# Forgetting attention of the prompt: spreading the inverse row sums by DRAM and GpSimd in place of TensorE and VectorE

## Chip, core and metric

The kernel runs on one core of one Trainium2 chip. The metric is device time in microseconds (us) of one execution; lower is better. TensorE is called PE, VectorE DVE, ScalarE ACT, GpSimd POOL and the queue that starts most of the transfers SP.

## What is computed

A two-layer decoder step for 2048 prompt tokens and 8 x 4 sample tokens. The change lies in layer 0, in the prompt's forgetting attention, with 8 heads of width 128. For one head and one block of 128 queries:

```python
s = (q_i @ k.T) * scale + (c_i[:, None] - c_keys[None, :])   # c: running sum of log forget gates
s = where(kpos <= qpos, s, -inf)
p = softmax(s, axis=-1)                                      # exp(s - max) / row sum
mix = p @ v
# later, for all heads:  b = concat(mix, memory_attention) * silu(gate);  x = x + rmsnorm(b @ w_out)
```

## The kernel before

The program is a row of stages: the input projection of layer 0 with much else run beside it, a barrier, the function `fox_attention` (lines 518 to 822), a barrier, the output projection, then layer 1. `fox_attention` holds all five engines; each runs its own list of instructions in order and waits on semaphores.

**The loop.** All engines walk the same steps x (`steps`, L562). Step x makes the scores of query block `qs` = x (128 queries; 16 blocks per head, 128 in all), transposes the probabilities of block `qt` = x-2, and multiplies with v for a pair J of query blocks (256 queries), one half of the keys per step: the product of pair J is made in steps 2J+4 and 2J+5. There are 8 pairs per head and 64 in all. A block q of a head sees q+1 blocks of keys, in pieces of 512 keys, so a head's first steps are short and its last are long.

- PE, in each step and piece: three matmuls for the scores (L700, L701, L702: high and low halves of q and k in fp32r), a mask matmul in the last piece (L704), its share of the product with v (L722, full fp32, two passes in the trace for each), then up to four transposes (L737, fp32). The scores go to four PSUM banks in turn.
- DVE: the decay row once in four blocks (L802), one add-and-max per piece out of PSUM (L811), the negated maximum (L816), and at the end of an even step x = 2J+2 the inverse of pair J's row sums (L821: `rr`, one number per query, the queries lying on the partitions, two columns).
- ACT: copies of the transposed probabilities (L762), the exponential with its row sum (L769), and the rounding of the next head's q and k (L750).
- SP: the transfers, in the order of L640 to L651. Stores and the next gate wait for DVE's `mix` (L624, L619), loads of q and k wait for the low halves (L601).
- POOL: the low halves of k (L663) and the work below.

**How the inverse gets to the gates.** The product lies with channels on the partitions and queries along the free axis, so it must be multiplied with 1/row sum along the free axis, the same in every partition. POOL writes a diagonal block from `ident` and `rr` (L670, `dg`), rounds it (L675, `dg_hi`) and takes the rest (L677, `dg_lo`). After the last L722 of a pair, PE multiplies a matrix of ones with both (L727, L728), which leaves the inverses in all 128 partitions of PSUM, in the second half of the bank of the product. At the start of step 2J+6 DVE multiplies the gate with this (L790) and then with the product (L795, `mix`). The buffers of `rr`, `gate`, `mix`, the transposed probabilities and the product are two deep.

```python
for x in range(NS_ + LAG + 2 * QB + 1):        # LAG = 2, QB = 2
    yield (x, qs, qt, product, pair(LAG), pair(LAG + 2 * QB))
```

Of the kernel before, what the change touches and what calls it, by code (L numbers as in the profile page):

```python
# [6 lines left out]
F32 = mybir.dt.float32  # L7
F32R = mybir.dt.float32r
# [506 lines left out]
    return Work(STEPS, plan, dict(sp=sp, pool=pool, pe=pe, act=act, dve=dve))  # L515


def fox_attention(nc, const, banks, zT, cT, bT, v_out):

# [2 lines left out]

    ident, ones_r, ident_b, mask_b = (const[n] for n in ("ident", "ones_r", "ident_b", "mask_b"))
    QB, NB, LAG, CK = 2, 3, 2, 4
    QW, CC = QB * P, 512
    NCH = NQ // QB  # L530
# [1 line left out]
    pieces = [(q + 4) // 4 for q in range(NQ)] * FH  # L532
    first = [sum(pieces[:n]) for n in range(NS_ + 1)]
    S_BANKS, T_BANKS = banks[0:4], banks[4:6]
    OUT = [(banks[6 + n][:, 0:QW], banks[6 + n][:, QW:2 * QW]) for n in range(2)]
    with ExitStack() as s:
        c = Core(nc, s, "fa")
        raws = [c.sb(f"{n}_raw", [P, 2, CC]) for n in "qk"]
# [6 lines left out]
        gate, mix = c.sb("gate", [P, 2, QW]), c.sb("mix", [P, 2, QW])  # L545
        mx, nm = c.sb("mx", [P, NB, 4]), c.sb("nm", [P, NB])
        rs, rr = c.sb("rs", [P, 2, QB]), c.sb("rr", [P, 2, QB])
        dg = c.sb("dg", [P, QB, P])
        dg_hi, dg_lo = (c.sb(n, [P, QB, P], F32R) for n in ("dg_hi", "dg_lo"))
        raw_in = [[c.sem(f"{n}_loaded{u}") for u in range(2)] for n in "qk"]  # L550
        v_in = [[c.sem(f"v{u}_loaded{ch}") for ch in range(CK)] for u in range(2)]
        hi_d, lo_d = [c.sem(f"{n}_hi_done") for n in "qk"], [c.sem(f"{n}_lo_done") for n in "qk"]
        c_in, dec_d = c.sem("c_loaded"), c.sem("decay_ready")
        g_in, mix_out = ([c.sem(f"{n}{u}") for u in range(2)] for n in ("gate_loaded", "mix_stored"))
        s_done, s_used, nm_d, p_done = (c.sem(n) for n in ("scores_done", "scores_used", "maxima_ready", "exp_done"))
        t_done, tc_d, rr_d = (c.sem(n) for n in ("p_transposed", "pT_copied", "row_inverse_ready"))
        dg_d, dgl_d, r_done, o_done = (c.sem(n) for n in ("diagonals_made", "diagonals_split", "inverse_spread", "pv_done"))
        gr_d, mix_d = c.sem("gate_scaled"), c.sem("mix_ready")
        block = s.enter_context(nc.Block())
        his, los = (q_hi, k_hi), (q_lo, k_lo)  # L560
# [1 line left out]
        def steps():  # L562

            for x in range(NS_ + LAG + 2 * QB + 1):
                pair = lambda lag: (x - lag) // QB if x >= lag and (x - lag) % QB == 0 and (x - lag) // QB < NJ else None
                yield (x, x if x < NS_ else None, x - LAG if LAG <= x < NS_ + LAG else None,
                       divmod(x - LAG - QB, QB) if LAG + QB <= x < NS_ + LAG + QB else None,  # L570
                       pair(LAG), pair(LAG + 2 * QB))

        def splits(x):

# [20 lines left out]
        def _(sp):  # L595
# [19 lines left out]
            def gates(J):  # L615
# [2 lines left out]
                    sp.wait_ge(mix_d, J - 1)  # L618
                sp.dma_start(gate[:, J % 2, :], zT[3 * D + XW + h * P:3 * D + XW + (h + 1) * P, QW * j:QW * (j + 1)]).then_inc(g_in[J % 2], 16)  # L619

            def store(J):
                h, j = divmod(J, NCH)
                sp.wait_ge(mix_d, J + 1)
                sp.dma_start(bT[h * P:(h + 1) * P, QW * j:QW * (j + 1)], mix[:, J % 2, :]).then_inc(mix_out[J % 2], 16)  # L624
# [12 lines left out]
                load_v(1, ch)  # L637
            for J in range(2):
                gates(J)
            for x, qs, qt, product, jr, jm in steps():  # L640
                for n, h, ch in splits(x - 1) if x else []:
                    i = CK * h + ch + 2
                    if i < CK * FH:
                        load(n, i // CK, i % CK)
                if qs is not None and qs % NQ == NQ - 2 and qs // NQ + 1 < FH:
                    decays(qs // NQ + 1)
                h, ch = divmod(x - LAG - 2 * QB - 1, NQ)
                if 1 <= h < FH - 1 and ch % 2 == 0 and ch // 2 < CK:
                    load_v(h + 1, ch // 2)
                if jm is not None:  # L650
                    store(jm)  # L651
                    if jm + 2 < NJ:
                        gates(jm + 2)
# [3 lines left out]
        @block.gpsimd  # L657
        def _(pool):
            def split(n, h, ch):
                i = CK * h + ch  # L660
                at = part(n, h, ch)
                pool.wait_ge(hi_d[n], i + 1)
                nc.gpsimd.tensor_tensor(los[n][at], raws[n][:, i % 2, :], his[n][at].bitcast(F32), ALU.subtract).then_inc(lo_d[n], 1)  # L663
            for n, h, ch in splits(-1):
                if n:
                    split(n, h, ch)
            for x, qs, qt, _, J, jm in steps():
                if J is not None:
                    pool.wait_ge(rr_d, J + 1)
                    nc.gpsimd.tensor_tensor(dg[:, :, :], ident[:, :].unsqueeze(1).broadcast_to([P, QB, P]),  # L670
                                            rr[:, J % 2, :].unsqueeze(2).broadcast_to([P, QB, P]), ALU.mult).then_inc(dg_d, 1)
                    pool.wait_ge(dg_d, 2 * J + 1)
                    if J:
                        pool.wait_ge(r_done, J)
                    nc.gpsimd.tensor_copy(dg_hi[:, :, :], dg[:, :, :]).then_inc(dg_d, 1)  # L675
                    pool.wait_ge(dg_d, 2 * J + 2)
                    nc.gpsimd.tensor_tensor(dg_lo[:, :, :], dg[:, :, :], dg_hi[:, :, :].bitcast(F32), ALU.subtract).then_inc(dgl_d, 1)  # L677
                    pool.wait_ge(dgl_d, J + 1)
                for n, h, ch in splits(x):
                    if n:  # L680
                        split(n, h, ch)

        @block.tensor
        def _(pe):
            for x, qs, qt, product, _, _ in steps():
                n_parts = max(1, parts(qs, qt))
                for p in range(n_parts):
                    if qs is not None and p < pieces[qs]:
# [17 lines left out]
                    if product is not None:  # L706
                        J, half = product
                        h, j = divmod(J, NCH)
                        n_keys = QB * (j + 1) // 2

                        late = 1 if half == 0 and n_parts > 1 else 0
                        at, of = max(0, p - late), n_parts - late
                        shared = range(n_keys * at // of, n_keys * (at + 1) // of) if p >= late else ()
                        for n in (n_keys * half + y for y in shared):
                            if n == 0:
                                if J >= 2:
                                    pe.wait_ge(mix_d, J - 1)
                                pe.wait_ge(tc_d, first[QB * (J + 1)])
                            if n % 4 == 0:
                                pe.wait_ge(v_in[h % 2][n // 4], 16 * (h // 2 + 1))  # L720
                            c0 = max(0, n - QB * j) * P
                            last = nc.tensor.matmul(OUT[J % 2][0][:, c0:QW], v[:, h % 2, n * P:(n + 1) * P], pT[:, J % 2, n, c0:QW],  # L722
                                                    start=(n == 0), stop=(n == QB * (j + 1) - 1))
                            if n == QB * (j + 1) - 1:
                                last.then_inc(o_done, 1)
                                pe.wait_ge(dgl_d, J + 1)
                                nc.tensor.matmul(OUT[J % 2][1], ones_r[:, :], dg_hi[:, :, :].rearrange("p a n -> p (a n)"), start=True, stop=False)  # L727
                                nc.tensor.matmul(OUT[J % 2][1], ones_r[:, :], dg_lo[:, :, :].rearrange("p a n -> p (a n)"),  # L728
                                                 start=False, stop=True).then_inc(r_done, 1)
                    if qt is not None and p < pieces[qt]:  # L730
                        g, q = first[qt] + p, qt % NQ
                        if p == 0:
# [9 lines left out]
        def _(act):  # L742
# [7 lines left out]
                nc.scalar.activation(his[n][part(n, h, ch)], raws[n][:, i % 2, :], ACT.Copy, scale=SCALE if n == 0 else 1.0).then_inc(hi_d[n], 1)  # L750
            for n, h, ch in splits(-1):
                split(n, h, ch)
            for x, qs, qt, _, _, _ in steps():
                if qt is not None:
                    q, J = qt % NQ, qt // QB
                    for p in range(pieces[qt]):
# [18 lines left out]
        def _(dve):  # L775
# [7 lines left out]
                if n == 0:  # L783
                    split(n, h, ch)
            n_dec = 0
            for x, qs, qt, _, jr, jm in steps():
                if jm is not None:
                    dve.wait_ge(r_done, jm + 1)
                    dve.wait_ge(g_in[jm % 2], 16 * (jm // 2 + 1))
                    nc.vector.tensor_tensor(gate[:, jm % 2, :], gate[:, jm % 2, :], OUT[jm % 2][1], ALU.mult).then_inc(gr_d, 1)  # L790
                    dve.wait_ge(gr_d, jm + 1)
                    dve.wait_ge(o_done, jm + 1)
                    if jm >= 2:
                        dve.wait_ge(mix_out[jm % 2], 16 * (jm // 2))
                    nc.vector.tensor_tensor(mix[:, jm % 2, :], gate[:, jm % 2, :], OUT[jm % 2][0], ALU.mult).then_inc(mix_d, 1)  # L795
                if qs is not None and qs % 4 == 0:
                    h, q = divmod(qs, NQ)
                    w = P * (q + 4)
# [18 lines left out]
                if jr is not None:  # L817
                    dve.wait_ge(p_done, QB * (jr + 1))
                    if jr >= 2:
                        dve.wait_ge(dg_d, 2 * (jr - 1))  # L820
                    nc.vector.reciprocal(rr[:, jr % 2, :], rs[:, jr % 2, :]).then_inc(rr_d, 1)  # L821
                for n, h, ch in splits(x):
                    if n == 0:
# [1472 lines left out]
def decoder_step(nc, ins, outs):  # L2296
# [14 lines left out]
    x1p, x1s = scratch("x1p", (SEQ, D)), scratch("x1s", (NS, D))  # L2311
    cT, sufT = scratch("cT", (FH, SEQ)), scratch("sufT", (DB * FH * TN, PAGES * P))
    cnew = scratch("cnew", (FH, NS))

    with ExitStack() as s:
        banks = [s.enter_context(nc.psum_tensor(f"bank{i}", [P, 512], F32)) for i in range(8)]
# [76 lines left out]
                project_pass(nc, "p0", const, banks, fox_w_in, halves, tiles, z0, bufs, rows,  # L2393
                             [making, norm, kv, sample, gates, fox, prompt, late], (page_table, cache_logf, past, ptab))
        nc.all_engine_barrier()
        fox_attention(nc, const, banks, z0, cT, bT, fox_v_p)
        output_projection(nc, "o0", banks, bT, w_out[0], norm_post[0], xp, xs, x1p, x1s)


# [45 lines left out]
```

## Time and profile before

| | |
|---|---|
| median of 3 runs | 3416.53 us (3413.59 to 3417.41) |
| the profiled execution: its own time | 3418.22 us |
| its span in the profile | 3416.6 us |
| stretch of `fox_attention`'s steps, from its first score to its last `mix` | 1464 to 2064 us |
| PE's busy time over the span | 3257.0 us |

Times in the rows are microseconds from the start of the span unless marked ns. "PEld" is PE's weight loads, which overlap the matmuls. A row "A <- B: t, n, m" of the waits says that A stood idle for t us in n times until B had finished, m at most. The ends of matmuls are modelled, so the distance from one start to the next is the better measure of what a matmul costs.

### The profile page before, as it was taken

The page shows a single profiled execution, that of the slowest core. Times are in us where ns is not written, and L with a number is a line of the kernel's source. Part 1 is how long each engine was busy: PE and PEld are TensorE (multiplying, and loading weights), DVE is VectorE, ACT ScalarE, POOL GpSimd, SP SyncE. Part 2 cuts the span into 40 slices and gives each one's busy share as a digit, 9 for nine tenths or more (in the row PEclk, how much of TensorE's full clock was granted, in tenths as well). Part 3 has the DMA queues.
Part 4 walks back from the last instruction along what each step waited for, and adds up shares of the span by engine and source line. Part 5 has one row for each costly group of instructions (what it writes and reads, how often), then busy time and mean ns, then how long its engine had stood idle before and what let it go on. Part 6 is the DMA issues. An engine that isn't in the chain of part 4 may idle for free. (4 is left out here: it accounts for less than half of the span.)

```text
span 3416.6 us, 51365 instructions
## 1 busy us (share of the span) xinstructions
PE 3257.0 (95%) x19697; PEld 2788.2 (82%) x19697; DVE 1302.6 (38%) x2583; ACT 1098.5 (32%) x2154; POOL 439.8 (13%) x643
## 2 busy tenths in 40 slices
PE   7999999899999999979999998997999999996999
PEld 7999999677777777768888886886999888775887
DVE  4331223232232215445555554223322246655332
ACT  3112232122222225355555553112223244112221
POOL 3310000101111112122222220000000012211000
PEclk9999999999999999989999999998999999998999
DMA  5444533579889964342232206332333444756431
GB/s 159 135 125 135 163 113 112 159 226 305 282 286 314 299 201 142 110 133 84 82 92 87 93 29 193 120 93 89 108 113 105 158 143 142 230 159 198 145 108 55
DMA packets 409059, 514.70 MB, mean 151 GB/s; under 512 B 50760, under 2 KB 298057, under 8 KB 407264
## 3 DMA queue, kind: packets, MB, share of 16 engines
q1 hardware_dynamic: 385975, 443.69, 41.7%
q0 software_dynamic: 22848, 67.78, 6.2%
q8 instruction: 158, 2.59, 0.3%
q14 instruction: 78, 0.63, 0.1%
HBM read 387.52 MB, written 124.22 MB: 150 GB/s over the span
## 5 line engine op out<-in xcount | busy, mean ns | idle before, releaser
L389 ACT ACTIVATE z_st_p<-bank 128x352 f32<-128x352 f32 (+3 forms) x325 | 168.5, 519 | 657.3 <-PE bank L364 657.0
L1522 PE MATMUL bank<-w_hi_o,b_hi_o 128*128 128x512 f32 x816 | 319.7, 392 | 26.9 <-DVE w_lo_o L1581 26.9
L364 PE MATMUL bank<-h00hi,w_hi_p 128*128 128x352 f32 x984 | 325.0, 330 | 4.8 <-DVE h00lo L1042 3.3
L1523 PE MATMUL bank<-w_hi_o,b_lo_o 128*128 128x512 f32 x816 | 318.9, 391 | 0.0
L1524 PE MATMUL bank<-w_lo_o,b_hi_o 128*128 128x512 f32 x816 | 318.9, 391 | 0.0
L364 PE MATMUL bank<-h00hi,w_lo_p 128*128 128x352 f32 x984 | 317.0, 322 | 0.0
L364 PE MATMUL bank<-h00lo,w_hi_p 128*128 128x352 f32 x984 | 316.7, 322 | 0.0
L722 PE MATMUL bank<-pT_fa,v_fa 128*128 128x256 f32 (+1 forms) x1152 | 291.4, 373 | 1.7 <-DVE mix_fa L795 0.7
L364 PE MATMUL bank<-h01hi,w_hi_p 128*128 128x512 f32 x656 | 274.2, 418 | 0.0
L364 PE MATMUL bank<-h01hi,w_lo_p 128*128 128x512 f32 x656 | 258.3, 394 | 0.0
L364 PE MATMUL bank<-h01lo,w_hi_p 128*128 128x512 f32 x656 | 257.2, 392 | 0.0
L321 DVE CAST w_hi_p<-w_raw_p 128x1024 fp32r<-128x1024 f32 (+1 forms) x130 | 89.3, 687 | 413.5 <-PE bank L364 413.4
L811 DVE CUSTOM_DVE_ANT_0 sc_fa<-bank,decay_fa 128x512 f32<-128x512 f32 (+2 forms) x320 | 189.1, 609 | 142.8 <-PE bank L704 82.6
L722 PEld LDWEIGHTS bank<-pT_fa,v_fa 128*128 128x128 f32 x1152 | 206.5, 191 | 28.9 <-DVE mix_fa L795 2.6
L762 ACT COPY pT_fa<-bank 128x512 f32<-128x512 f32 (+2 forms) x320 | 164.2, 518 | 203.5 <-PE bank L737 203.5
L1980 DVE COPY kT_sf<-bank 128x512 f32<-128x512 f32 x128 | 88.6, 692 | 354.2 <-PE bank L1908 354.1
L1522 PEld LDWEIGHTS bank<-w_hi_o,b_hi_o 128*128 128x128 f32 x816 | 154.1, 189 | 61.0 <-DVE w_lo_o L1581 27.8
L364 PEld LDWEIGHTS bank<-h00hi,w_hi_p 128*128 128x128 f32 x984 | 185.6, 189 | 10.4 <-issue 4.9
L364 PE MATMUL bank<-h10hi,w_hi_p 128*128 128x352 f32 x576 | 188.1, 327 | 3.1 <-DVE h10lo L1042 3.1
L364 PEld LDWEIGHTS bank<-h00lo,w_hi_p 128*128 128x128 f32 x984 | 186.0, 189 | 0.6
L364 PE MATMUL bank<-h10lo,w_hi_p 128*128 128x352 f32 x576 | 185.7, 322 | 0.0
L364 PE MATMUL bank<-h10hi,w_lo_p 128*128 128x352 f32 x576 | 185.7, 322 | 0.0
(290 smaller groups left out, 6588.3 us busy)
## 6 DMA issues: line engine op xcount, KB each, us to landing
k_raw_sf<-in_cache_fox_k SPq DMA_DIRECT2D x128, 512.0 KB, 5.4
v_raw_sf<-in_cache_fox_v POOLq DMA_DIRECT2D x128, 512.0 KB, 5.8
z<-z_st_p SPq DMA_DIRECT2D x112, 512.0 KB, 2.8
w_raw_p<-in_fox_w_in SPq DMA_DIRECT2D x80, 512.0 KB, 5.2
b_raw_o<-bT SPq DMA_DIRECT2D x32, 768.0 KB, 6.5
w_raw_p<-in_pool_w_in SPq DMA_DIRECT2D x48, 512.0 KB, 5.0
out<-tok_p SPq DMA_DIRECT2D x64, 256.0 KB, 4.3
w_raw_o<-in_w_out SPq DMA_DIRECT2D x24, 512.0 KB, 4.5
```

The lines of the kernel that those rows point to most:

```text
L321: nc.vector.tensor_copy(w_hi[:, u, :, 0:width], w_raw[:, u, :, 0:width]).then_inc(whi_d, 1)
L364: last = nc.tensor.matmul(bank[:, 0:width], wt[:, u, k, :], h[:, k, at0:at0 + width], start=(m == 0), stop=(m == MM - 1))
L389: nc.scalar.activation(z_st[0:rows_t, t % 2, at0:at0 + width], bank[0:rows_t, 0:width], tiles[t][2]).then_inc(z_read, 1)
L722: last = nc.tensor.matmul(OUT[J % 2][0][:, c0:QW], v[:, h % 2, n * P:(n + 1) * P], pT[:, J % 2, n, c0:QW], start=(n == 0), stop=(n == QB * ...
L762: nc.scalar.copy(pT[:, J % 2, 4 * p:4 * p + nk, a * P:(a + 1) * P], T_BANKS[g % 2][:, 0:nk * P].rearrange("p (n q) -> p n q", q=P)).then_i ...
L811: nc.vector.tensor_tensor_reduce(out=sc[:, b, k0:k0 + w], in0=S_BANKS[g % 4][:, 0:w], in1=decay[:, k0:k0 + w], scale=1.0, scalar=LOWEST, o ...
L1522: nc.tensor.matmul(bank(t, half)[:, :], bh, w_hi[:, k, cols], start=(k == 0), stop=False)
L1523: nc.tensor.matmul(bank(t, half)[:, :], bl, w_hi[:, k, cols], start=False, stop=False)
L1524: last = nc.tensor.matmul(bank(t, half)[:, :], bh, w_lo[:, k, cols], start=False, stop=(k == NK - 1))
L1980: nc.vector.tensor_copy(kT[:, s // 2 % 2, 4:8, s % 2 * P:(s % 2 + 1) * P], T_BANKS[1][:, :].rearrange("p (h n) -> p h n", h=4)).then_inc(k ...
```

## The change

`rr` is stored to a new DRAM scratch `inverses` (8 x 2048) in 256 runs of 4 bytes (step 2J+3, SP), read back as a row of 1 KB into each of the 128 partitions (step 2J+4, SP, behind a wait for the store's landing), and POOL multiplies the gate with it in SBUF (step 2J+5). DVE keeps L795 alone. The three diagonal instructions, the two matmuls with ones and DVE's gate multiply go.

```diff
-    OUT = [(banks[6 + n][:, 0:QW], banks[6 + n][:, QW:2 * QW]) for n in range(2)]
+    OUT = [banks[6 + n][:, 0:QW] for n in range(2)]
...
+        r_bc = c.sb("r_bc", [P, 2, QW])
...
-                       pair(LAG), pair(LAG + 2 * QB))
+                       pair(LAG), pair(LAG + 2 * QB), pair(LAG + 1), pair(LAG + 2), pair(LAG + 3))
...
+            def store_inverse(J):
+                h, j = divmod(J, NCH)
+                sp.wait_ge(rr_d, J + 1)
+                sp.dma_start(inverses[h, QW * j:QW * (j + 1)].rearrange("(a p) -> p a", p=P), rr[:, J % 2, :],
+                             allow_slow_non_contiguous=True).then_inc(r_out[J % 2], 16)
+
+            def spread_inverse(J):
+                h, j = divmod(J, NCH)
+                sp.wait_ge(r_out[J % 2], 16 * (J // 2 + 1))
+                if J >= 2:
+                    sp.wait_ge(gr_d, J - 1)
+                sp.dma_start(r_bc[:, J % 2, :], inverses[h, QW * j:QW * (j + 1)].partition_broadcast(P)).then_inc(r_in[J % 2], 16)
...
-            for x, qs, qt, product, jr, jm in steps():
+            for x, qs, qt, product, jr, jm, ji, jb, _ in steps():
+                if ji is not None:
+                    store_inverse(ji)
+                if jb is not None:
+                    spread_inverse(jb)
...
-                    pool.wait_ge(rr_d, J + 1)
-                    nc.gpsimd.tensor_tensor(dg[:, :, :], ident..., rr..., ALU.mult).then_inc(dg_d, 1)
-                    pool.wait_ge(dg_d, 2 * J + 1)
-                    if J:
-                        pool.wait_ge(r_done, J)
-                    nc.gpsimd.tensor_copy(dg_hi[:, :, :], dg[:, :, :]).then_inc(dg_d, 1)
-                    pool.wait_ge(dg_d, 2 * J + 2)
-                    nc.gpsimd.tensor_tensor(dg_lo[:, :, :], dg[:, :, :], dg_hi..., ALU.subtract).then_inc(dgl_d, 1)
-                    pool.wait_ge(dgl_d, J + 1)
+                    pool.wait_ge(g_in[J % 2], 16 * (J // 2 + 1))
+                    pool.wait_ge(r_in[J % 2], 16 * (J // 2 + 1))
+                    nc.gpsimd.tensor_tensor(gate[:, J % 2, :], gate[:, J % 2, :], r_bc[:, J % 2, :], ALU.mult).then_inc(gr_d, 1)
...
                                 last.then_inc(o_done, 1)
-                                pe.wait_ge(dgl_d, J + 1)
-                                nc.tensor.matmul(OUT[J % 2][1], ones_r[:, :], dg_hi..., start=True, stop=False)
-                                nc.tensor.matmul(OUT[J % 2][1], ones_r[:, :], dg_lo..., start=False, stop=True).then_inc(r_done, 1)
...
-                    dve.wait_ge(r_done, jm + 1)
-                    dve.wait_ge(g_in[jm % 2], 16 * (jm // 2 + 1))
-                    nc.vector.tensor_tensor(gate[:, jm % 2, :], gate[:, jm % 2, :], OUT[jm % 2][1], ALU.mult).then_inc(gr_d, 1)
                     dve.wait_ge(gr_d, jm + 1)
                     dve.wait_ge(o_done, jm + 1)
...
-                        dve.wait_ge(dg_d, 2 * (jr - 1))
+                        dve.wait_ge(r_out[jr % 2], 16 * (jr // 2))
                     nc.vector.reciprocal(rr[:, jr % 2, :], rs[:, jr % 2, :]).then_inc(rr_d, 1)
```

## Rows read from the trace of the kernel before

**Rows 1.** The page: busy time of each engine over the span.
```profile
PE 3257.0 (95%) x19697; PEld 2788.2 (82%) x19697; DVE 1302.6 (38%) x2583; ACT 1098.5 (32%) x2154; POOL 439.8 (13%) x643
```

**Rows 2.** Busy time by stretch; last columns: granted PE clock, DMA share, GB/s.
```profile
1464.00:1500.00 36.00, 27.89 (x158) 23.22 (x159) 21.10 (x72) 21.46 (x45) 13.59 (x18) 0.81 0.57 176
1600.00:1700.00 100.00, 99.22 (x590) 84.60 (x589) 50.33 (x162) 55.30 (x106) 25.20 (x37) 1.00 0.27 79
```

**Rows 3.** Waits from 1464 to 2065 us.
```profile
DVE gate_fa L790 <- PE bank L728: 50.3, 24, 7.5
...
PE bank L737 <- ACT pT_fa L762: 3.2, 6, 0.5
```

**Rows 4.** Groups of instructions by line and shape, 1464 to 2065 us.
```profile
L677 POOL TENSOR_TENSOR dg_lo_fa<-dg_fa,dg_hi_fa 128x256 fp32r<-128x256 f32 x64 | 49.1, 767 | 5.1
...
L728 PE MATMUL bank<-dg_lo_fa,ones_r_const 128*128 128x256 f32 x64 | 18.1, 283 | 0.0
```

**Rows 5.** Timeline, PE: a pair's end before transposes, and a stretch without it.
```profile
2043.61 0.87 PE L722 MATMUL bank<-pT_fa,v_fa 128*128 128x256 f32 x4
...
2044.24 0.36 PE L727 MATMUL bank<-dg_hi_fa,ones_r_const 128*128 128x256 f32 x1
...
2044.56 0.82 PE L737 MATMUL bank<-ident_const,sc_fa 128*128 128x128 f32 x6
...
2052.17 1.03 PE L722 MATMUL bank<-pT_fa,v_fa 128*128 128x256 f32 x4
...
2053.04 0.60 PE L737 MATMUL bank<-ident_const,sc_fa 128*128 128x128 f32 x4
```

**Rows 6.** Timeline, PE: product before scores, without the two matmuls and with them.
```profile
1551.45 0.65 PE L722 MATMUL bank<-pT_fa,v_fa 128*128 128x256 f32 x2
...
1552.17 0.40 PE L701 MATMUL bank<-k_hi_fa,q_lo_fa 128*128 128x512 f32 x1
...
1553.51 0.44 PE L722 MATMUL bank<-pT_fa,v_fa 128*128 128x128 f32 x2
...
1554.26 0.40 PE L701 MATMUL bank<-k_hi_fa,q_lo_fa 128*128 128x512 f32 x1
```

**Rows 7.** Timeline, second head: inverses and mixes of pairs 9 and 10, POOL's k split.
```profile
1552.97 0.17 DVE L821 RECIPROCAL rr_fa<-rs_fa 128x2 f32<-128x2 f32 x1
...
1558.14 1.28 POOL L663 TENSOR_TENSOR k_lo_fa<-k_raw_fa,k_hi_fa 128x512 fp32r<-128x512 f32 x1 [2.27 <-ACT k_hi_fa L750]
...
1558.42 0.17 DVE L821 RECIPROCAL rr_fa<-rs_fa 128x2 f32<-128x2 f32 x1
...
1561.32 0.42 DVE L795 TENSOR_TENSOR mix_fa<-gate_fa,bank 128x256 f32<-128x256 f32 x1
...
1569.21 0.42 DVE L795 TENSOR_TENSOR mix_fa<-gate_fa,bank 128x256 f32<-128x256 f32 x1
```

**Rows 8.** DMA issues of the whole run: count, KB each, median us to landing.
```profile
c_bc_fa<-cT SPq DMA_DIRECT2D x8, 1024.0 KB, 5.4
...
gate_fa<-z SPq DMA_DIRECT2D x64, 128.0 KB, 2.2
bT<-mix_fa SPq DMA_DIRECT2D x64, 128.0 KB, 2.8
...
sc_col_pm<-in_pool_scale SPq DMA_DIRECT2D x1, 4.0 KB, 7.9
```

**Rows 9.** Timeline: the end of the stage.
```profile
2062.39 0.36 PE L727 MATMUL bank<-dg_hi_fa,ones_r_const 128*128 128x256 f32 x1
...
2062.91 0.42 DVE L790 TENSOR_TENSOR gate_fa<-gate_fa,bank 128x256 f32<-128x256 f32 x1 [7.46 <-PE bank L728]
2063.36 0.42 DVE L795 TENSOR_TENSOR mix_fa<-gate_fa,bank 128x256 f32<-128x256 f32 x1
```

**Rows 10.** Timeline, start of the stage: inverse and mix of pair 0, DVE.
```profile
1475.34 0.17 DVE L821 RECIPROCAL rr_fa<-rs_fa 128x2 f32<-128x2 f32 x1
...
1483.20 0.42 DVE L795 TENSOR_TENSOR mix_fa<-gate_fa,bank 128x256 f32<-128x256 f32 x1
```

More of the change, by code:

```diff
@@ L515, in prompt_gates, with fox_attention @@
     return Work(STEPS, plan, dict(sp=sp, pool=pool, pe=pe, act=act, dve=dve))
-def fox_attention(nc, const, banks, zT, cT, bT, v_out):
-    ident, ones_r, ident_b, mask_b = (const[n] for n in ("ident", "ones_r", "ident_b", "mask_b"))
+def fox_attention(nc, const, banks, zT, cT, bT, inverses, v_out):
+    ident, ident_b, mask_b = (const[n] for n in ("ident", "ident_b", "mask_b"))
     QB, NB, LAG, CK = 2, 3, 2, 4
@@ L547, in fox_attention @@
         rs, rr = c.sb("rs", [P, 2, QB]), c.sb("rr", [P, 2, QB])
-        dg = c.sb("dg", [P, QB, P])
-        dg_hi, dg_lo = (c.sb(n, [P, QB, P], F32R) for n in ("dg_hi", "dg_lo"))
+        r_bc = c.sb("r_bc", [P, 2, QW])
         raw_in = [[c.sem(f"{n}_loaded{u}") for u in range(2)] for n in "qk"]
@@ L555, in fox_attention @@
         s_done, s_used, nm_d, p_done = (c.sem(n) for n in ("scores_done", "scores_used", "maxima_ready", "exp_done"))
-        t_done, tc_d, rr_d = (c.sem(n) for n in ("p_transposed", "pT_copied", "row_inverse_ready"))
-        dg_d, dgl_d, r_done, o_done = (c.sem(n) for n in ("diagonals_made", "diagonals_split", "inverse_spread", "pv_done"))
+        t_done, tc_d, rr_d, o_done = (c.sem(n) for n in ("p_transposed", "pT_copied", "row_inverse_ready", "pv_done"))
+        r_out, r_in = ([c.sem(f"{n}{u}") for u in range(2)] for n in ("inverse_stored", "inverse_spread"))
         gr_d, mix_d = c.sem("gate_scaled"), c.sem("mix_ready")
@@ L666, in _ @@
                     split(n, h, ch)
-            for x, qs, qt, _, J, jm in steps():
+            for x, qs, qt, _, _, _, _, _, J in steps():
                 if J is not None:
-                    pool.wait_ge(rr_d, J + 1)
-                    nc.gpsimd.tensor_tensor(dg[:, :, :], ident[:, :].unsqueeze(1).broadcast_to([P, QB, P]),
-                                            rr[:, J % 2, :].unsqueeze(2).broadcast_to([P, QB, P]), ALU.mult).then_inc(dg_d, 1)
-                    pool.wait_ge(dg_d, 2 * J + 1)
-                    if J:
-                        pool.wait_ge(r_done, J)
-                    nc.gpsimd.tensor_copy(dg_hi[:, :, :], dg[:, :, :]).then_inc(dg_d, 1)
-                    pool.wait_ge(dg_d, 2 * J + 2)
-                    nc.gpsimd.tensor_tensor(dg_lo[:, :, :], dg[:, :, :], dg_hi[:, :, :].bitcast(F32), ALU.subtract).then_inc(dgl_d, 1)
-                    pool.wait_ge(dgl_d, J + 1)
+                    pool.wait_ge(g_in[J % 2], 16 * (J // 2 + 1))
+                    pool.wait_ge(r_in[J % 2], 16 * (J // 2 + 1))
+                    nc.gpsimd.tensor_tensor(gate[:, J % 2, :], gate[:, J % 2, :], r_bc[:, J % 2, :], ALU.mult).then_inc(gr_d, 1)
                 for n, h, ch in splits(x):
@@ L684, in _ @@
         def _(pe):
-            for x, qs, qt, product, _, _ in steps():
+            for x, qs, qt, product, *_ in steps():
                 n_parts = max(1, parts(qs, qt))
@@ L721, in _ @@
                             c0 = max(0, n - QB * j) * P
-                            last = nc.tensor.matmul(OUT[J % 2][0][:, c0:QW], v[:, h % 2, n * P:(n + 1) * P], pT[:, J % 2, n, c0:QW],
+                            last = nc.tensor.matmul(OUT[J % 2][:, c0:QW], v[:, h % 2, n * P:(n + 1) * P], pT[:, J % 2, n, c0:QW],
                                                     start=(n == 0), stop=(n == QB * (j + 1) - 1))
@@ L725, in _ @@
                                 last.then_inc(o_done, 1)
-                                pe.wait_ge(dgl_d, J + 1)
-                                nc.tensor.matmul(OUT[J % 2][1], ones_r[:, :], dg_hi[:, :, :].rearrange("p a n -> p (a n)"), start=True, stop=False)
-                                nc.tensor.matmul(OUT[J % 2][1], ones_r[:, :], dg_lo[:, :, :].rearrange("p a n -> p (a n)"),
-                                                 start=False, stop=True).then_inc(r_done, 1)
                     if qt is not None and p < pieces[qt]:
@@ L752, in _ @@
                 split(n, h, ch)
-            for x, qs, qt, _, _, _ in steps():
+            for x, qs, qt, *_ in steps():
                 if qt is not None:
@@ L785, in _ @@
             n_dec = 0
-            for x, qs, qt, _, jr, jm in steps():
+            for x, qs, qt, _, jr, jm, *_ in steps():
                 if jm is not None:
-                    dve.wait_ge(r_done, jm + 1)
-                    dve.wait_ge(g_in[jm % 2], 16 * (jm // 2 + 1))
-                    nc.vector.tensor_tensor(gate[:, jm % 2, :], gate[:, jm % 2, :], OUT[jm % 2][1], ALU.mult).then_inc(gr_d, 1)
                     dve.wait_ge(gr_d, jm + 1)
@@ L794, in _ @@
                         dve.wait_ge(mix_out[jm % 2], 16 * (jm // 2))
-                    nc.vector.tensor_tensor(mix[:, jm % 2, :], gate[:, jm % 2, :], OUT[jm % 2][0], ALU.mult).then_inc(mix_d, 1)
+                    nc.vector.tensor_tensor(mix[:, jm % 2, :], gate[:, jm % 2, :], OUT[jm % 2], ALU.mult).then_inc(mix_d, 1)
                 if qs is not None and qs % 4 == 0:
@@ L2313, in decoder_step @@
     cnew = scratch("cnew", (FH, NS))
+    inverses = scratch("inverses", (FH, SEQ))
     with ExitStack() as s:
@@ L2395, in decoder_step @@
         nc.all_engine_barrier()
-        fox_attention(nc, const, banks, z0, cT, bT, fox_v_p)
+        fox_attention(nc, const, banks, z0, cT, bT, inverses, fox_v_p)
         output_projection(nc, "o0", banks, bT, w_out[0], norm_post[0], xp, xs, x1p, x1s)
```

## The prediction, made before the changed kernel ran

> **What bounds the kernel now.** I read the page first: PE is busy 95% of the span, no other engine over 38% [rows 1]. Then the table by stretch, since a share of the whole says nothing of one stage. In the attention steps PE is busy 99.2 of 100 us at the full clock, DVE 50, ACT 55, POOL 25, and the DMA share is 0.27 [rows 2]; four further stretches of 100 us look the same. Only the first 36 us are looser (27.9 busy, clock 0.81) [rows 2]. Third, the waits of this stage: the longest waits of DVE for what the change touches, 50.3 us [rows 3], are waits of an idle engine for PE. PE itself waits 3.2 us in six times for ACT's copies, all in short steps [rows 3], and about 8 us once, at the start. So the stage is one long stream of matmuls. What leaves that stream is gained; what leaves DVE and POOL is not, except at the end, where nothing runs beside them.
>
> **What goes from PE.** 64 times L727 and 64 times L728, 283 ns each of the latter [rows 4]. Busy times overlap their neighbours', so I take distances between starts. What follows the two differs.
>
> *Transposes follow (5 of 8 pairs of a head, 40 in all).* From the last run of L722 (two passes of 256 columns and two of 128) to the transposes: 2044.56 - 2043.61 = 0.95 us; L727 begins at 0.63 of it [rows 5]. Without the two, four passes of 256 columns need 2053.04 - 2052.17 = 0.87 us [rows 5], 0.217 each, so the run with half-width passes would need 3 x 0.217 = 0.65. The two matmuls cost 0.95 - 0.65 = 0.30 us.
>
> *Scores follow (3 of 8, 24 in all).* From a half-width L722 over both matmuls and L700 to L701: 1554.26 - 1553.51 = 0.75 us. The nearest case without them has a full-width L722: 1552.17 - 1551.45 = 0.72 us [rows 6]; the half width takes 0.217 off, 0.50. So 0.25 us. It is less than 0.30 because fp32r matmuls start late behind fp32 ones: now L727 pays that, afterwards L700 does.
>
> Sum: the 64th pair is the end of the stage, counted below; 39 x 0.30 + 24 x 0.25 = 11.7 + 6.0 = 17.7 us. As bounds: 0.20 for each (a spacing that the remaining stream gives back in part) makes 12.6, 0.32 for each (start of L727 to start of L737 [rows 5]) 20.2.
>
> **What goes from DVE.** L790, 64 times 0.42 us [rows 9]. It is hidden behind PE and I cost it at nothing; the step's first add-and-max starts some 0.75 us sooner against PE, which can only shrink the 3.2 us of [rows 3].
>
> **The end of the stage.** Nothing covers it. Now: L727 at 2062.39, L790 at 2062.91, L795 at 2063.36 [rows 9]. Afterwards L795 can start when the last L722 is drained, which ends by its neighbours some 0.25 us after 2062.39. So 2063.36 - 2062.64 = 0.7 us. The inverse of that pair is made over 15 us before and will be long there.
>
> **What is added, and whether it stays hidden.** Per pair: a store of 1 KB in 256 runs of 4 bytes, a spread of 128 KB, and one POOL multiply.
> - The multiply: nearest row L677, same size, two inputs in SBUF, 767 ns [rows 4]. POOL loses three instructions for it.
> - The spread: the same bytes and row length as `gate`, 2.2 us; bound above by `c_bc`, eight times larger, 5.4 us [rows 8].
> - The store: bounds are 2.2 us (below, the gate's row) and 7.9 us, the only row with 4-byte runs, `sc_col`, four times as many and issued behind 1.5 MB of loads [rows 8]. I take 2.8, the store of `mix` [rows 8]: that one moves 128 times the bytes, and 16 short runs per engine are few.
> - Issue on SP: about 0.4 us for each of the two.
>
> The Trainium skill speaks against the store: "DMA: Bandwidth & Descriptors", section Specifications, wants at least 512 B per transfer for line rate and says that below it the engines read, modify and write. By that rule this store is of the worst kind. It gives no time, and in this trace I see none for a store of 4-byte runs.
>
> The chain from inverse to gate is then 0.1 + 0.4 + 2.8 + 0.4 + 2.2 + 0.8 = 6.7 us. The room is the time from the end of L821 to L795 of the same pair. It is smallest for the second pair of a head: 1561.32 - 1553.14 = 8.2 us [rows 7]; I walked all 64 pairs: the third of a head has 1569.21 - 1558.59 = 10.6 us [rows 7], the others more; the last head's second has somewhat less room, but no k split before it. POOL does its k split, 1558.14 to 1559.42 [rows 7], ahead of that multiply, so the gate is ready at about 1560.2, just in time. If it comes late, DVE waits at the head of the step with its add-and-max queued behind it; PE goes on through four score banks, and its transposes use blocks two steps old. I put that slack at about 4 us (two short steps of some 2.2 us).
>
> SP's queue: `store_inverse` of J waits for an inverse that DVE makes at the end of the step whose `mix` SP has just stored, so nothing useful is held. `spread_inverse` holds SP for the store's 2.8 us; behind it stand loads of q and k (needed some 7 steps later), the store of the last `mix` (its buffer is needed four steps later) and the next gate (needed three steps later). For pair 10 I get the gate ready at about 1566.8 against 1568.6. No stall.
>
> **The start** is the place where it fails to fit. SP still issues loads of v and gates until 1479, under a DMA share of 0.57 [rows 2]. The first inverse is ready at 1475.5, its `mix` runs at 1483.20 [rows 10]. With the store issued at 1479.0, landing at 1481.7, the spread landing near 1484.6 and the multiply, the gate is there at 1485.4, 2.2 us late. PE's slack covers most of it: I charge 0.5 us, with 0 to 3 as bounds.
>
> **Sum.** 17.7 + 0.7 - 0.5 = 17.9 us; I round it down by half a us for the short steps, where PE waits for ACT anyway, to 17.4. The profiled execution's 3418.22 becomes 3400.8. Its time lies 1.7 us above the median of the runs, 3416.53, so the median becomes 3399.1. About 0.2% (6.8 us) is what a measurement of this kernel can tell from no change; this is 0.51%.
>
> **Rivals.**
> 1. *The short steps are paced by ACT and DVE, not by PE.* Speaks for it: PE's waits for L762 lie there. Against: they sum to 3.2 us in the whole stage, and the chain through DVE gets shorter by more than PE's. Three of eight pairs end in short steps; if theirs is given back, 24 x 0.27 = 6.5 us is lost: 3405.6. Chance 0.12.
> 2. *A slower chain with part of the gain.* Store 5 us, spread 3: 9.7 us against 8.2, DVE late by 1.5 us or more at the second and third pair of each head, and the slack is less than I put it: PE loses about 1 us per head and 2 more at the start, 3399.1 + 10 = 3409. Chance 0.08.
> 3. *Slower: the round trip through DRAM paces the head's first steps.* One mechanism: 4-byte stores land like `sc_col` and the spread like `c_bc`. Chain 0.1 + 0.4 + 7.9 + 0.4 + 5.4 + 1.3 + 0.8 = 16.3 us against 8.2, late by 8.1, of which 4 are slack: 4 us in the second pair; SP is held for 8 us per pair and the third pair, with 10.6 us of room, is late too, some 2 us beyond slack. 6 x 8 = 48 us lost against 17.9 gained: 3447. It decides the sign once the chain is longer than 8.2 + 4 + 17.9/8 = 14.4 us. The trace speaks against it: the DMA share is low and `gate` lands in 2.2 us. This is also how the page's rule would make itself felt; since so few runs are stored, I give it 0.04.
> 4. *The matmuls' places are not gained at all* (the stream is held by weight loads or by the sequencer, so that two fewer change nothing): 3416. PEld is busy 84.6 of 100 us [rows 2], so it isn't the limit. Chance 0.04.
>
> The forecast has the rest, 0.72.
>
> **Range.** Its own spread is 3396.5 (0.32 us for each) to 3404 (0.20). Down to 3395.5 for a gain on PE's waits for ACT, up to 3407 for rival 1 and the start of rival 2: left out are rivals 3, 4 and most of 2. Faster by over 0.2%: forecast, rival 1 and most of 2, 0.90; within 0.2%: rival 4 and the rest of 2, 0.06; slower 0.04.
>
> **What would show it.** L795 of the last pair about 17 us earlier against the stage's first score; PE busy 99% in the same stretches; the period of a head down by 2.2 us; the store landing in 2 to 3.5 us; the second pair's `mix` waiting less than 1 us for POOL. I am wrong if PE shows new idle time at the blocks 6 to 10 of each head, released by ACT or DVE (rivals 2, 3), or if the head's period shrinks by under 1.5 us with PE at 99% (rival 4 or a wrong price for the two matmuls).

## The result, and the profile after

| | before | changed |
|---|---|---|
| median | 3416.95 us | 3617.12 us (3611.33 to 3625.12, 4 runs) |
| profiled execution, span | 3416.6 us | 3617.6 us |

The ratio is 1.0595, 95% interval [1.0582, 1.0608]: 200 us slower, where 17 us faster was forecast.

The page first. The columns are busy time, share of the span and instructions.

```profile
PE 3308.1 (91%) x19569; PEld 2812.3 (78%) x19569; DVE 1263.3 (35%) x2519; ACT 1097.3 (30%) x2154; POOL 371.0 (10%) x515
PEclk9999999999999999788889898899899999997999
```

The 128 matmuls, 64 DVE and 128 POOL instructions are gone, as against [rows 1], but PE's share fell and the granted clock has dips in the attention's slices. The table by stretch of the changed kernel (PE, PEld, DVE, ACT, POOL, clock, DMA share, GB/s) says where:

```profile
1600.00:1700.00 100.00, 79.39 (x413) 65.12 (x414) 34.94 (x120) 42.95 (x80) 10.32 (x12) 0.88 0.55 68
```

In the same stretch PE did 590 matmuls before at clock 1.00 [rows 2], now 413. No engine took its place: all are idle more. The DMA share doubled to 0.55 while the GB/s fell from 79 to 68. So engines wait, and transfers occupy the DMA engines without moving much. The waits of this stage (A <- B: us in total, times, longest), then those of SP's queue:

```profile
POOL gate_fa L687 <- DMA r_bc_fa<-inverses: 698.9, 63, 17.0
DVE mix_fa L797 <- POOL gate_fa L687: 385.7, 62, 10.4
ACT sc_fa L774 <- DVE nm_fa L818: 291.3, 76, 11.5
...
PE bank L709 <- DVE mx_fa L813: 136.8, 38, 9.2
```

```profile
SPq L631 <- DMA inverses<-rr_fa: 588.2, 63, 12.2
SPq L600 <- DVE q_lo_fa L785: 5.0, 2, 4.5
SPq L600 <- POOL k_lo_fa L679: 3.5, 3, 1.7
```

Read from the bottom: SP stood 588 us waiting for stores of the inverses to land (L631 starts the spread); POOL waited for the spread, DVE for POOL, ACT and PE for DVE. SP's waits for the low halves, 8.5 us here, were these in the kernel before:

```profile
SPq L601 <- DVE q_lo_fa L780: 136.8, 28, 7.0
SPq L601 <- POOL k_lo_fa L663: 134.0, 29, 6.6
```

SP is no longer early for anything. PE pays twice. It stands idle, and after an idle time it runs at a lower granted clock: 0.53 from 1806.5 to 1809.4 us, close to the lower of its two levels (1.2 of 2.4 GHz), after 4.4 us without work. The same matmul (L710, 512 columns) at that clock and 4 us later:

```profile
1807.00 0.63 PE L710 MATMUL bank<-k_hi_fa,q_lo_fa 128*128 128x512 f32 x1
...
1810.74 0.39 PE L710 MATMUL bank<-k_hi_fa,q_lo_fa 128*128 128x512 f32 x1
```

The issues of transfers in the stage (count, KB each, median us to landing):

```profile
gate_fa<-z SPq DMA_DIRECT2D x64, 128.0 KB, 8.7
r_bc_fa<-inverses SPq DMA_DIRECT2D x63, 128.0 KB, 5.0
bT<-mix_fa SPq DMA_DIRECT2D x62, 128.0 KB, 8.9
...
inverses<-rr_fa SPq DMA_DIRECT2D x64, 1.0 KB, 10.6
```

One KB needs 10.6 us, and the transfers around it are slow too: `gate` needs 8.7 us, 2.2 before [rows 8]. SP's timeline shows the turn of its list:

```profile
1797.62 0.32 SPq L631 DMA_DIRECT2D r_bc_fa<-inverses  x1
...
1802.37 0.49 SPq L623 DMA_DIRECT2D inverses<-rr_fa  x1
1802.91 0.47 SPq L607 DMA_DIRECT2D v_fa<-out  x1
1811.08 0.33 SPq L631 DMA_DIRECT2D r_bc_fa<-inverses  x1
1811.46 0.43 SPq L636 DMA_DIRECT2D bT<-mix_fa  x1
1811.93 0.43 SPq L618 DMA_DIRECT2D gate_fa<-z  x1
1812.40 0.45 SPq L623 DMA_DIRECT2D inverses<-rr_fa  x1
```

From 1803.4 to 1811.1 SP does nothing. The moment the store has landed it starts the spread, the last product's store, the next gate and at once the next store, whose inverse is long there. The gate is started half a us ahead of the store (1811.93 and 1812.40) and not behind it; it is so with 30 of the 32 gates whose landing the trace tells, and none of the 32 was started while a store was under way. The store holds up what was started just before it as well.

The first `mix` of the stage is at 1491.87, the last at 2268.14: 776.3 us for 63 intervals, 12.3 us per pair, in short steps nearly as in long ones (means of 11.4 to 14.0 us by the pair's place in its head). Before, the pairs took 4.2 to 13.6 us by the length of their steps, 9.2 on average.

### The profile page after: what moved, and what is told of

Read it like the earlier page. It is cut to its first block and busy times, and to the rows that moved or that the text cites. A ratio compares the mean times of both kernels' runs of the same rounds, so it can differ in the third digit from the quotient of the medians.

```text
span 3617.6 us, 50980 instructions
## 1 busy us (share of the span) xinstructions
PE 3308.1 (91%) x19569; PEld 2812.3 (78%) x19569; DVE 1263.3 (35%) x2519; ACT 1097.3 (30%) x2154; POOL 371.0 (10%) x515
## 5 line engine op out<-in xcount | busy, mean ns | idle before, releaser
L731 PE MATMUL bank<-pT_fa,v_fa 128*128 128x256 f32 (+1 forms) x1152 | 307.9, 389 | 1.7 <-issue 0.7
L709 PE MATMUL bank<-k_hi_fa,q_hi_fa 128*128 128x512 f32 (+2 forms) x320 | 159.2, 497 | 150.6 <-DVE mx_fa L813 136.8
L731 PEld LDWEIGHTS bank<-pT_fa,v_fa 128*128 128x128 f32 x1152 | 217.7, 201 | 32.2 <-issue 2.6
L774 ACT ACTIVATE sc_fa<-sc_fa,nm_fa 128x128 f32<-128x128 f32 (+15 forms) x128 | 154.2, 1205 | 291.5 <-DVE nm_fa L818 291.3
L742 PE MATMUL bank<-ident_const,sc_fa 128*128 128x128 f32 x1088 | 187.4, 291 | 18.3 <-ACT sc_fa L774 9.4
L709 PEld LDWEIGHTS bank<-k_hi_fa,q_hi_fa 128*128 128x128 f32 x320 | 68.7, 215 | 164.6 <-DVE mx_fa L813 115.6
```

What stands on the lines that cost most here:

```text
L709: nc.tensor.matmul(out, qh, k_hi[:, h % 2, k0:k0 + w], start=True, stop=False)
L731: last = nc.tensor.matmul(OUT[J % 2][:, c0:QW], v[:, h % 2, n * P:(n + 1) * P], pT[:, J % 2, n, c0:QW], start=(n == 0), stop=(n == QB * (j ...
L742: last = nc.tensor.transpose(T_BANKS[g % 2][:, n * P:(n + 1) * P], sc[:, qt % NB, (4 * p + n) * P:(4 * p + n + 1) * P], ident[:, :])
L774: nc.scalar.activation(sc[:, qs % NB, 0:w], sc[:, qs % NB, 0:w], ACT.Exp, bias=nm[:, qs % NB:qs % NB + 1], accum_out=rs[:, J % 2, qs % QB: ...
```

## Experiments

Two questions. **Why does the store need 10.6 us**: the number of runs, their place in DRAM, or a wait behind other transfers? **Through whom does it cost**: SP's held queue (theory H), the longer chain from inverse to gate (rival R), or the load on the DMA engines (rival C)? Each ratio below is against the kernel before on the same chip.

### Without the store

```diff
-                sp.wait_ge(r_out[J % 2], 16 * (J // 2 + 1))
+                sp.wait_ge(rr_d, J + 1)
...
-                sp.dma_start(r_bc[:, J % 2, :], inverses[h, ...].partition_broadcast(P))...
+                sp.dma_start(r_bc[:, J % 2, :], cT[h, ...].partition_broadcast(P))...
```

> Leaves out the store of the inverses: the spread reads rows of cT instead, so the gates are scaled with wrong numbers; the spread, POOL's multiply and the rest stay. Theory S (the landing of the store, 10.6 us in the trace, for which SP waits with its queue behind it, makes the loss): the time falls to what was predicted, 3399 us, within 4; spreads land in 2.2 us. Rival Q (the spread, POOL's multiply or SP's longer list cost the time whatever the store does): over 3416.

3396.23 us, ratio 0.9944 [0.9928, 0.9961]. All else of the change stays and is worth about what was forecast: 18.6 us against the kernel before on the same chip, 17.4 forecast. The spread landed in 3.9 us, not 2.2, and DVE waited only 0.6 us in all for the scaled gates. The loss comes with the store and the wait for it.

### Runs of 8 bytes

```diff
-inverses[h, ...].rearrange("(a p) -> p a", p=P)
+inverses[h, ...].rearrange("(p a) -> p a", p=P)
```

> The same 1 KB stored as 128 runs of 8 bytes (both queries of a partition side by side in DRAM); POOL reads the spread row in steps of two. Theory S by number of runs: the landing halves to about 5.5 us and the time to 3440 or less. Theory L (what costs is that many engines write into the same 1 KB of DRAM, run by run): the same, 5.5 us. Rival F (the landing is a wait behind other transfers of the queue): unchanged, 10 us and 3617.

3408.26 us, ratio 0.998 [0.997, 0.999]; the store lands in 4.9 us, `gate` in 4.6. The expectation had 3440 or less. Half the runs, less than half the landing; rival F falls. SP still waits 202 us for the store. Number and place are not yet told apart.

### The same runs, apart

```diff
-inverses[h, ...].rearrange("(a p) -> p a", p=P), rr[:, J % 2, :],
+inverses[h, ...].rearrange("(a p s) -> p a s", p=P, s=P)[:, :, 0:1], rr[:, J % 2, :].unsqueeze(2),
```

> Still 256 runs of 4 bytes, but each into a block of 512 bytes of its own in a scratch 128 times as large; the spread waits for it as before but reads a row of cT, so the gates are scaled with wrong numbers. Theory S by number of runs: as the changed kernel, 10 us and 3617. Theory L (writes into the same 1 KB stand in line): the landing falls to about 3 us and the time to about 3402.

3397.82 us, ratio 0.9955 [0.994, 0.9971]. Two closer spacings, s=16 and s=8:

> As the run with the 4-byte runs 512 bytes apart, but 64 bytes apart (a pair's inverses in 16 KB of DRAM); the spread reads rows of cT again, so the gates are scaled with wrong numbers. If the runs stand in line only where they fall into the same 64 bytes: landing near 3 us, time near 3398. If into the same 512 bytes or the same few KB: landing 5 to 10 us, time 3410 to 3617.

> As the run with the 4-byte runs 64 bytes apart, now 32 bytes apart, two in each 64 bytes; the spread reads rows of cT, so the gates are scaled with wrong numbers. If the runs stand in line where they fall into the same 64 bytes, and two per line are few: landing 2.8 to 3.5 us, 3397 to 3402. If a wider block counts: landing over 4 us.

One execution each: 3399.31 us and 3400.53 us. The row of the store was the same in the three kernels; the one with the closest spacing, 32 bytes, beside its `gate`:

```profile
gate_fa<-z SPq DMA_DIRECT2D x64, 128.0 KB, 2.3
...
inverses<-rr_fa SPq DMA_DIRECT2D x64, 1.0 KB, 2.8
```

256 runs of 4 bytes land in 2.8 us, exactly the price taken in the prediction, if each has 32 bytes to itself; eight runs to 32 bytes take 10.6 us, four of 8 bytes 4.9 us. So neither the size nor the number of the runs is slow, but their lying side by side. Theory L holds, in a narrower block than I had expected: 32 bytes apart is enough, and spacings between 8 and 32 bytes were not run, so the width of the block stays open. These three kernels don't read the stored words back; the run with the transpose, below, does.

The trace's records of single DMA packets say where the time is. The 4-byte packets take 9 ns each, crowded or 512 bytes apart (median, and no more in nine of ten). The packets of other transfers are stretched: those of 1 KB (gates, `mix`, spreads) take 139 ns on average in the stage of the changed kernel and 53 with the words 512 bytes apart, those of 512 bytes 78 and 29.

The Trainium skill's rule ("DMA: Bandwidth & Descriptors", Specifications: under 512 B the engines read, modify and write) agrees with the crowded store and would also have condemned the one with 32 bytes between the runs, which lands like a store of 128 KB. That crowded writes wait for one another's read and write back would fit both, but no run shows the mechanism itself.

### The target in SBUF

```diff
-sp.dma_start(inverses[h, ...].rearrange("(a p) -> p a", p=P), rr[:, J % 2, :], ...)
+for a in range(QB):
+    sp.dma_start(row[0:1, J % 2, P * a:P * (a + 1)], rr[:, J % 2, a:a + 1], ...)
```

> The whole computation. The same 256 runs of 4 bytes, in two transfers, go to a row of one partition in SBUF and the spread reads that row; no DRAM. If it is DRAM that makes small writes stand in line: landing 2 to 3 us; the spread reads 128 KB out of one partition and may take 3 to 6 us; time 3397 to 3410. Rival N (the count of runs costs, whatever the target): landing 8 us or more, 3550 or more.

3426.35 us, ratio 1.0038 [1.0024, 1.0051]; the 4-byte writes land in 3.5 us though they are crowded, the spread out of one partition in 6.7 us and `gate` in 6.3. Rival N falls: side by side in SBUF the words are not slow, so the 10.6 us need the target in DRAM. (Two things changed, the target and one transfer made into two; no run has the two transfers to DRAM.) The loss against the other kernels without a slow store is another one, by its rows the spread of 128 KB out of a single partition: it needs more than the 3 to 6 us expected, and DVE waited 83.5 us for POOL's multiply. That it is the spread which slows `gate` here was not run by itself.

### An unused store in the kernel before

```diff
+                if x % QB == 1 and 0 <= (x - LAG - 1) // QB < NJ:
+                    store_inverse((x - LAG - 1) // QB)     # rr four deep, nobody waits but its fourth successor
```

> The kernel before, with the store of 256 runs of 4 bytes added at the same place of SP's list and nobody waiting for its landing (the inverses have four buffers). Theory W (the wait on SP is what costs): 3417 to 3420. Rival C (the slow store holds up the other transfers too, as gate's landing of 8.7 us in the changed kernel suggests): gate lands in 6 us or more, and the time rises to 3425 or more.

3415.23 us, ratio 1.0007 [0.9997, 1.0017]. Here is what it does to the others, in this kernel:

```profile
gate_fa<-z SPq DMA_DIRECT2D x64, 128.0 KB, 8.9
bT<-mix_fa SPq DMA_DIRECT2D x63, 128.0 KB, 8.6
...
inverses<-rr_fa SPq DMA_DIRECT2D x64, 1.0 KB, 9.4
```

Half of each theory: the other transfers are held up as much as in the changed kernel (C's mechanism), yet the time doesn't move (W's time). The transfers start early enough here, because SP doesn't wait: in the whole stage DVE waits 8.2 us for gates.

### The wait moved to POOL

```diff
-                if jb is not None:
-                    spread_inverse(jb)
...
+                    pool.wait_ge(r_out[J % 2], 16 * (J // 2 + 1))
+                    pool.dma_start(r_bc[:, J % 2, :], inverses[h, ...].partition_broadcast(P))...
```

> The changed kernel with one thing moved: the wait for the store's landing and the start of the spread go from SP to POOL, ahead of its multiply; the store stays as it is (256 runs of 4 bytes in 1 KB) and SP waits for no landing. Theory H (SP, held for some 10 us per pair with stores, gates and the next inverse behind it, turns at 12 us per pair whatever the length of the steps): most of the loss goes, 3400 to 3440, and what is left lies at the first pairs of a head, which have 8 to 14 us of room. Rival R (the chain from the inverse to the gate, 10.6 + 5 + 0.8 us, is too long wherever it runs): 3550 or more.

3509.2 us, ratio 1.0281 [1.0257, 1.0305]: between the two expectations, so it decided nothing. Its waits from 1464 to 2065 us, the last one SP's, show why:

```profile
POOL gate_fa L683 <- DMA r_bc_fa<-inverses: 289.6, 54, 9.4
DVE mix_fa L793 <- POOL gate_fa L683: 193.2, 38, 11.4
POOL r_bc_fa L680 <- DMA inverses<-rr_fa: 190.8, 27, 13.9
...
SPq L600 <- POOL k_lo_fa L670: 228.5, 29, 12.6
```

POOL now waits for the landing of the store and then for that of the spread before it multiplies, and DVE waits for POOL: that is rival R's chain. POOL's splits of k come late as well, so that SP waits 228.5 us for them before it reloads the buffer, 134.0 in the kernel before: that may hold SP's queue again. The run has both and doesn't tell them apart.

### DVE without the inverse, and the wait two pairs later

DVE multiplies product and gate when the product is there; POOL multiplies the result with the inverse in step 2J+9, and SP stores it in step 2J+10. The buffers of `rr`, `mix` and the spread row are four deep. The second kernel differs from the first in one number, the step in which SP waits for the store and starts the spread.

```diff
-pair(LAG + 1), pair(LAG + 2), pair(LAG + 3))
+pair(LAG + 1), pair(LAG + 2), pair(LAG + 7), pair(LAG + 8))     # first kernel
+pair(LAG + 1), pair(LAG + 6), pair(LAG + 7), pair(LAG + 8))     # second kernel
...
+nc.vector.tensor_tensor(mix[:, jm % 4, :], gate[:, jm % 2, :], OUT[jm % 2], ALU.mult)
...
+nc.gpsimd.tensor_tensor(mix[:, J % 4, :], mix[:, J % 4, :], r_bc[:, J % 4, :], ALU.mult)
```

> The whole computation, the slow store as in the changed kernel, SP waiting for it at the same place of its list (step 2J+4). But DVE multiplies product and gate as soon as the product is there, without the inverse, and POOL multiplies the result with it in step 2J+9; so no engine but POOL waits for the inverse. Theory H (what costs is SP's queue, held some 10 us per pair, 12 us for a turn of its list, with the gates and loads of q, k and v behind): gates reach DVE late, 3560 to 3620. Rival R (the wait of DVE for the inverse's own way through DRAM costs): 3396 to 3410. Both in part, as the run with the spread on POOL has it: 3450 to 3550.

> As the run before, and the wait and the spread stand two pairs later in SP's list (step 2J+8), when the store has landed by itself; so nobody waits for it. Theories H and R agree: 3396 to 3412 with the slow store still in place, which shows that it costs only by who waits. Rival C (its load on the DMA engines costs PE's other transfers): over 3420.

3590.34 us, ratio 1.0514 [1.0495, 1.0533], and 3397.46 us, ratio 0.9954 [0.9939, 0.9969]. The rows of the first kernel:

```profile
DVE mix_fa L797 <- DMA gate_fa<-z: 229.4, 47, 12.1
...
SPq L631 <- DMA inverses<-rr_fa: 541.4, 60, 12.1
```

and of the second, for the same product:

```profile
DVE mix_fa L797 <- PE bank L731: 45.2, 16, 7.7
...
DVE mix_fa L797 <- DMA gate_fa<-z: 17.2, 7, 5.7
```

In the first, DVE no longer needs the inverse, and 173 of the 200 us are still lost: now it waits for gates that SP starts too late. In the second, SP passes the same crowded stores without standing still, and all of the loss is gone with a gain of 0.46% on top. The other transfers are slow in it as before (loads of v land in 10.1 us, 3.8 in the kernel before; the trace doesn't tell the store's own landing), so rival C falls too. **The 193 us between them are the place of one wait in SP's list.** Rival R alone falls; it can account for some 27 us of the changed kernel, the difference of 3617 and 3590, and only roughly, since the two kernels differ in more than this wait.

### The store as eight runs of 128 bytes

DVE, idle half the time, transposes the inverses in blocks of 32 x 32, so that 32 of them lie in one partition.

```diff
+                    nc.vector.transpose(rt[:, jr % 2, :], rr[:, jr % 2, :]).then_inc(rr_d, 1)
...
+                for a in range(QB):
+                    at = QW * j + P * a
+                    sp.dma_start(inverses[h, at:at + P].rearrange("(b c) -> b c", c=32), rt[a:a + 97:32, J % 2, :])...
```

> The whole computation. DVE transposes the inverses in blocks of 32 x 32 before the store, so that it goes out as 8 runs of 128 bytes in two transfers; the rest as in the changed kernel. If many small writes into one place are the whole cause: store landing 2 to 2.5 us, the first 3396 to 3403 us, 0.4 to 0.6% under the kernel before. Rival Q (something else of the changed path still costs): over 3408, as with runs of 8 bytes.

3399.55 us, ratio 0.9959 [0.9945, 0.9973], the full computation. The stretch, to be held against [rows 2] and the changed kernel's row above:

```profile
1600.00:1700.00 100.00, 99.71 (x588) 84.67 (x587) 49.89 (x173) 58.54 (x113) 14.47 (x16) 1.00 0.32 95
```

The groups show what it added and what POOL's multiply costs:

```profile
L689 POOL TENSOR_TENSOR gate_fa<-gate_fa,r_bc_fa 128x256 f32<-128x256 f32 x64 | 48.8, 762 | 263.1 <-DMA r_bc_fa<-inverses 262.9
...
L829 DVE STREAM_TRANSPOSE rt_fa<-rr_fa 128x32 f32<-128x32 f32 x64 | 13.6, 212 | 2.4 <-DVE rr_fa L827 0.2
```

212 ns on an idle engine buy back everything. The trace doesn't tell the landing of the store's two transfers; SP waits 56.3 us for them in the whole stage, 2.5 at most, against 588.2 in the changed kernel. The transpose was also combined with the later scaling:

> The whole computation. DVE's 32 x 32 transpose before the store, and DVE's multiply without the inverse as in the first of these runs. Against the run with the transpose alone it can gain only the late first pairs, 1 to 3 us: 3396 to 3399. If those are not late enough to matter: 3399.5, the same.

3399.6 us, ratio 0.9954 [0.994, 0.9967]: the same as the transpose alone to what the runs can tell. In the profiles the late start is gone: from the first inverse to the `mix` of pair 7 it takes 74.1 us, with the transpose alone 77.9. Those 3.8 us, 0.1% of the whole, are not to be seen in the medians.

## Why the prediction was wrong

By its own steps:

- **What bounds the kernel, and what goes from PE: right, the sum in part by luck.** In the run with the transpose a whole head takes (1977.49 - 1550.79) / 6 = 71.12 us from `mix` to `mix`, before (1991.94 - 1550.50) / 6 = 73.57. That is 2.46 us against the forecast 2.2. What is left without the two matmuls can be read there directly, before scores and before transposes, as the successors of [rows 6] and [rows 5]:

```profile
1554.19 0.44 PE L733 MATMUL bank<-pT_fa,v_fa 128*128 128x128 f32 x2
...
1554.70 0.39 PE L712 MATMUL bank<-k_hi_fa,q_lo_fa 128*128 128x512 f32 x1
...
2037.96 0.82 PE L733 MATMUL bank<-pT_fa,v_fa 128*128 128x256 f32 x4
2038.61 0.60 PE L744 MATMUL bank<-ident_const,sc_fa 128*128 128x128 f32 x4
```

  0.51 us where 0.50 was forecast, and 0.65 where 0.65 was. But the six waits of PE for L762 [rows 3] are one of 0.53 us in each of six heads, and in this run none of them is left (the row's 1.4 us here are one wait in the stage's start). The prediction took them at nothing in its sum. So of the 2.46 us 0.53 come from this wait and 1.93 from the two matmuls, less than the 2.2 forecast: not every pair gives back the full price, and the two errors nearly cancel.
- **The multiply (0.8 us) and the issue: right**; 762 ns. **The spread:** 2.2 us forecast, 3.0 to 3.9 measured without a slow store, 5.0 in the changed kernel, above the row I took but inside its bounds.
- **The store: this step failed.** I took 2.8 us and a bound of 7.9; it needs 10.6. The bound came from the only row with 4-byte runs, `sc_col`, and that is a load. A load of such runs says nothing of a store of them, and I let it close the range from above. I also read "16 short runs per engine are few" where what counts is that they lie side by side: 32 bytes apart, as many words land in the 2.8 us that I took.
- **SP's queue: failed with it.** "`spread_inverse` holds SP for the store's 2.8 us" was the right question with a wrong number; with 10.6 the same sentence gives a turn of the list of 12 us, longer than the average pair, 9.2. This should have been worked out as a rate, landing plus issues against the time per pair, and not only as a delay for single pairs. The size alone doesn't explain the miss: with the measured landings the chain is 0.1 + 0.4 + 10.6 + 0.4 + 5.0 + 0.8 = 17.3 us, and by rival 3's own rule for the sign that costs 8 x (17.3 - 14.4) = 23 us, where 200 were lost.
- **Rival 3 named the mechanism** and the right sign, at 3447. Its price was low since it lengthened the chain and let slack of 4 us absorb it in all but two pairs per head. A queue that turns at 12.3 us per pair has no slack anywhere: 63 x (12.3 - 9.2) = 195 us. It had 0.04 of the chance because the trace showed a low DMA share and a fast `gate`, and neither says anything of 4-byte stores. With the term unmeasured it deserved several times that. The Trainium skill's rule ("DMA: Bandwidth & Descriptors", Specifications), which the prediction names against this store, spoke for more as well.
- **The start** was to cost 0.5 us, at most 3. With the transpose it cost 3.8, by the comparison with the run that also scales later (77.9 against 74.1 us). DVE waited 3.5 us for the first gate where I had reckoned 2.2, and PE's slack did not cover it: from 1480 to 1500 us PE was busy 18.4 us at a granted clock of 0.91, against 20.0 us at 1.00 in the other run.
- **The forecast time**, 3399.1, is what the change gives once the store is out of the way: 3396.2, 3397.8 and 3399.6 us without a crowded store, 3397.5 with one for which nobody waits. Against the kernel before on the same chip these are gains of 18.6, 17.0, 14.3 and 17.1 us, 17.4 forecast; the first two kernels leave out part of the computation.

## What to carry to other kernels

A blocking wait for a DMA's landing in a queue that also starts everything else turns a latency into a rate: compare landing plus issues with the time per turn before asking who needs the data, and put such a wait so late in the list that it finds the transfer landed. Don't scatter single words next to each other into DRAM from many partitions; transpose them first into runs on an idle engine, or leave 32 bytes for each. A price for a store needs a row of a store.

## What was not expected of the hardware

- 256 runs of 4 bytes, stored to DRAM in one transfer, land in 2.8 us when 32, 64 or 512 bytes apart and in 10.6 us when side by side; half as many, twice as long ones, side by side, in 4.9 us.
- A crowded 1 KB store holds up unrelated transfers of the same queue, those started half a us ahead of it too: `gate` lands in 8.9 us instead of 2.2, without a change of the kernel's time as long as nobody waits with the queue in hand.
- The crowded words' own packets take 9 ns each, as the spaced ones do; the packets of the other transfers are stretched. Why was not tried: whether it lies in the DRAM's write path or in the DMA engines' treatment of neighbouring words.
